# Laying HGRN's work slots as one list over two pairs of heads, and weighting slot positions by chunk

## The reference

```python
h = rms_norm(x, norm_mix) * (1.0 + sc_a) + sh_a
z = h @ w_in
q, k, v, rq, rf, ri, rg, ga, gr = split(z)
...
o_attn = sliding_window_attention(q, k, v)      # 16 heads, 4 kv heads, window 128, sinks, ALiBi
o_rec, s_new = hgrn2_chunked(qr, kr, vr, logf, s0)   # 8 heads, 128x128 state each
mixed = sigmoid(ga) * o_attn + sigmoid(gr) * o_rec
x = x + g_a * (mixed @ w_out)
x = x + g_m * (square(relu(h2 @ w_up)) @ w_down)
```

## Time and profile before

| | |
|---|---|
| time, median of 3 runs | 1206.25 us (1203.26 to 1206.48) |
| the profiled execution | 1207.19 us, span of its instructions 1205.4 us |
| TensorE | busy 1136.0 us (94% of the span), mean granted clock 0.972 |
| VectorE, ScalarE, GpSimd | busy 706.4, 530.5, 174.1 us |
| stretch that holds the slots | about 94 us to 674 us of the span |

### The profile page before, as it was taken

The page is one execution under the profiler, slowest core; times in us unless marked ns, Lnnn a source line. Parts: engine busy times, 40 slices in busy tenths (PEclk is TensorE's granted clock), DMA queues, the critical chain, the costliest instruction groups (busy, mean ns, idle before and its releaser), DMA issues.

```text
span 1205.4 us, 22012 instructions
## 1 busy us (share of the span) xinstructions
PE 1136.0 (94%) x8837; PEld 1073.0 (89%) x8837; DVE 706.4 (59%) x1437; ACT 530.5 (44%) x939; POOL 174.1 (14%) x137
## 2 busy tenths in 40 slices
PE   5798999997999989999999999799999999999997
PEld 4687889885899988989999999589999999999997
DVE  5635555545386677376688654744553744636465
ACT  3432556466546555555536423443323233232324
POOL 1300000000142123122031001231001010110101
PEclk9899999998999989999999999799999999999999
DMA  9684432312232312213222265112222222232212
GB/s 301 201 302 154 136 106 71 107 36 70 109 94 73 108 38 71 72 50 95 76 68 73 91 236 157 36 46 95 71 96 80 72 87 89 71 104 71 71 36 79
DMA packets 108779, 120.46 MB, mean 100 GB/s; under 512 B 2693, under 2 KB 98653, under 8 KB 108390
## 3 DMA queue, kind: packets, MB, share of 16 engines
q1 hardware_dynamic: 108677, 119.06, 30.4%
HBM read 109.22 MB, written 11.80 MB: 100 GB/s over the span
## 4 chain that ended last, share of the span: by engine, by line
PE 44%; DVE 4%; ACT 1%; issue 1%; POOL 0%; DVEq 0%; ACTq 0%; POOLq 0%
PE PS L834 40%; DVE wR L1408 1%; DVE tmp L1392 1%; DVE xhat L1376 1%; PE PS L956 0%; PE PS L747 0%; PE PS L1002 0%; PE PS L1019 0%; PE PS L780 0%; DVE tmp L1391 0%; DVE xT L1425 0%; PE PS L843 0%; ACT wR L1079 0%; DVE xT L1426 0%; PE PS L986 0%
## 5 line engine op out<-in xcount | busy, mean ns | idle before, releaser
L834 PE MATMUL PS<-hR,wR 128*128 128x288 f32 x3744 | 530.9, 300 | 0.8 <-issue 0.8
L834 PEld LDWEIGHTS PS<-hR,wR 128*128 128x128 f32 x3744 | 508.1, 190 | 10.3 <-issue 9.5
L834 PE MATMUL PS<-actR,wR 128*128 128x288 f32 (+2 forms) x1920 | 259.3, 295 | 1.8 <-DVE actR L1556 1.8
L834 PEld LDWEIGHTS PS<-actR,wR 128*128 128x128 f32 x1920 | 255.5, 188 | 3.0 <-DVE actR L1556 2.0
L1408 DVE TENSOR_TENSOR wR<-raw,wR 128x512 fp32r<-128x512 f32 x256 | 209.1, 817 | 81.1 <-ACT wR L1079 74.1
L1079 ACT ACTIVATE wR<-raw 128x512 fp32r<-128x512 f32 x256 | 161.8, 632 | 140.5 <-PE PS L834 132.9
L1741 POOL TENSOR_TENSOR D<-b 128x512 f32<-128x512 f32 (+1 forms) x48 | 60.4, 1257 | 490.6 <-PE PS L921 263.6
L1471 DVE CAST actR<-tmp 128x576 fp32r<-128x576 f32 x32 | 15.2, 476 | 129.5 <-ACT tmp L1190 129.5
L1768 POOL TENSOR_TENSOR actR<-tmp,actR 128x576 fp32r<-128x576 f32 x32 | 46.3, 1448 | 304.7 <-DVE actR L1471 304.7
L789 PE MATMUL PS<-wR,hR 128*128 128x256 f32 x600 | 80.6, 292 | 2.2 <-ACT kT L1159 2.2
L789 PEld LDWEIGHTS PS<-wR,hR 128*128 128x128 f32 x600 | 75.8, 196 | 4.7 <-ACT kT L1159 2.4
(11 more groups left out here) (223 smaller groups left out, 1233.3 us busy)
## 6 DMA issues: line engine op xcount, KB each, us to landing
raw<-in_w_in SPq DMA_DIRECT2D x30, 1024.0 KB, 5.1
raw<-in_w_up SPq DMA_DIRECT2D x16, 1024.0 KB, 5.5
raw<-in_w_down SPq DMA_DIRECT2D x16, 1024.0 KB, 5.0
mid<-in_w_ada SPq DMA_DIRECT2D x12, 1024.0 KB, 5.0
ada<-in_w_ada SPq DMA_DIRECT2D x8, 1024.0 KB, 12.4
S<-in_state_hgrn SPq DMA_DIRECT2D x8, 512.0 KB, 4.2
out_hgrn_sample<-S SPq DMA_DIRECT2D x8, 512.0 KB, 5.0
raw<-in_w_out SPq DMA_DIRECT2D x4, 1024.0 KB, 5.3
```

The costliest lines, as they stand in the source:

```text
L834: mm = pe.matmul(PS[:, 2 * x.pair + h, 0:size], weights(x, w, k, col), rhs[r], start=(k == 0 and n == 0), stop=(k == last and n == 2))
```

## The change

The function that lays slots now counts room: a chunk has room 2, a chunk of a unit of kind ri has room 1, and slots are spread evenly over the sum of the room. The HGRN slots of pairs 0 and 1 are laid as one list over ga 0 to ri 2, those of pairs 2 and 3 as one list over rf 3 to rg 2. The slots, their events and their order stay as they are.

```diff
-        slots, chunks = list(slots), [(x.t, c) for x in TILES[begin:end] if x.u not in MID for c in range(parts(x))]
-        for n, ev in enumerate(slots):
-            plan.setdefault(chunks[n * len(chunks) // len(slots)], []).extend(ev)
+        slots, at = list(slots), 0
+        chunks = [(x, c) for x in TILES[begin:end] if x.u not in MID for c in range(parts(x))]
+        room = [1 if x.kind == "ri" and CHUNKS.get("ri") == 2 else 2 for x, _ in chunks]
+        for (x, c), r in zip(chunks, room):
+            for n in range(-(-at * len(slots) // sum(room)), -(-(at + r) * len(slots) // sum(room))):
+                plan.setdefault((x.t, c), []).extend(slots[n])
+            at += r
...
     spread(attention_slots(), first["q", 1], first["ga", 0])
-    spread(hgrn_slots(0), first["ga", 0], first["rf", 2])
-    spread(hgrn_slots(1), first["rf", 2], first["rf", 3])
-    spread(hgrn_slots(2), first["rf", 3], first["gr", 1])
-    spread(hgrn_slots(3), first["gr", 1], first["gr", 3])
+    spread([*hgrn_slots(0), *hgrn_slots(1)], first["ga", 0], first["rf", 3])
+    spread([*hgrn_slots(2), *hgrn_slots(3)], first["rf", 3], first["gr", 3])
```

## The result

The kernel after takes 1223.82 us in the median of 4 runs (1223.73 to 1224.08), against 1206.37 us (1203.26 to 1209.05) before in the same comparison: a ratio of 1.015, 95% interval 1.013 to 1.017. It is slower, by 17 us. The forecast was 1203.8 us, so it was wrong, and the range did not hold the time.

What follows compares the result with a forecast made beforehand. TensorE bounds the kernel, so only waits and granted clock can change. Attention +2.5, heads 0 to 3 -4.0 and heads 4 to 7 -1.0 sum to -2.5 us: 1203.8 us, own range 1200 to 1210, 8-in-10 range 1196.5 to 1212.5.

Steps and rivals of the forecast that it cites:

- the guest at 30.1: Attention: slots follow each other at 28.2 and 28.3 and 30.0 is now empty, so this guest waits 1.5 us more.
- the first sample step: Attention: it moves from 31.3 to 31.0, before `q_blocks` has ended, and TensorE waits 1.0 us more.
- tile 43: Attention, rf 1 and rq 1: with one slot more, waits of about 2.0, 0.7 and 0.9 us here.
- The two waits of the earlier trace: Heads 0 to 3: the waits of 2.73 us at 63.2 and 2.04 us at 66.1 both go.
- levels 1, 2, 3 of head 1: Heads 0 to 3, in ga at 57.1 to 57.3, all with `lo`: a new wait of 1.5 us.
- levels 2 to 4 of head 2: Heads 0 to 3, at 61.1 to 61.3, again with `lo`: a new wait of 1.0 us.
- head 3 behind the scans: Heads 0 to 3: head 3 stands behind the scans of rf 2, a new wait of 1.0 us.
- The rate 1.5: Heads 0 to 3: the 1.5 us charged for three neighbouring levels with `lo` in ga, the shape of 66.1.
- I move 2 of the 2.7 us: Heads 4 to 7: of the 2.67 us wait at 73.0, 2 us pass from level 3 of head 4 to level 4.
- Head 7's wait: Heads 4 to 7: head 7 starts at 87.2, with the merge and `lo` in the same chunk, and may wait 2 us.
- Waits move, the sum stays: First rival, the forecast itself: removed waits have near twins, time within -3.6 and +3.6 us; chance 0.42.
- Rival 3: Slower: attention's loop no longer catches up in rf and rq, +8.5 us, 1214.8 us; chance 0.22.

Runs made afterwards that it cites:

- e1: Kernel after with attention's slots laid as before (equal room), HGRN's as changed: 1219.58 us, ratio 1.0122 to the kernel before.
- e2: Kernel after with HGRN's slots laid as before, attention's still weighted: 1210.23 us, ratio 1.0034 to the kernel before.
- e5: Kernel after with one slot, level 5 of head 4, moved one chunk later from 73.1 to 73.2: 1216.78 us, ratio 1.0086 to the kernel before.
- e3: Kernel after with the joined HGRN lists kept but equal room for every chunk, attention too: 1216.21 us, ratio 1.0087 to the kernel before.
- e4: Kernel after with four separate HGRN lists, ri still at room 1, attention at equal room: 1208.39 us, ratio 1.002 to the kernel before.
- e6: Kernel after with attention and pairs 2 and 3 as before, pairs 0 and 1 separate and weighted: 1202.44 us, ratio 0.996 to the kernel before.
- e7: Kernel after with attention and pairs 2 and 3 as before, pairs 0 and 1 joined with equal room: 1205.91 us, ratio 0.9993 to the kernel before.
- e8: Plan of the kernel before with the slots of pairs 2 and 3 one chunk later: 1209.85 us, ratio 1.0025 to the kernel before.
- e11: Plan of the kernel before with all attention slots one chunk later, room equal: 1209.26 us, ratio 1.0035 to the kernel before.
- e9: Pairs 0 and 1 separate and weighted, rest as before, plus three slots at waits (73.0, 85.1, 88.0) one chunk later: 1203.18 us, ratio 0.998 to before.
- e10: Kernel after with five slots of heads 1 to 3, at or right behind its large waits, one chunk later: 1223.58 us, ratio 1.0146 to the kernel before.

## Why the prediction was wrong

**Bound.** That only waits and clock can change was right: the constant part of each stretch is the same before and after, to 0.6 us. SyncE's transfers, costed at nothing, cost nothing: no wait of TensorE in these stretches ends with a transfer, before or after. That one wait more counts nearly double, because of the clock, does not hold for the sum: 15.7 us of waits came with 1.7 us of clock.

**Attention, +2.5 forecast, +3.9 measured.** The mechanism was right, the list of waits was short, and part of the agreement is luck: waits were to rise by 1.5 us and rose by 7.1, while the clock, put at 1.0 us of loss more, lost 3.4 us less. As forecast, TensorE waits at 22.0 (2.67 for 3.08 us, gain 0.4 of 0.5), the guest at 30.1 waits (1.33 against 1.5), the first sample step waits (0.63 against 1.0), tile 43 waits (2.25, 0.93, 1.34 against 2.0, 0.7, 0.9), the guest of tile 45 waits (1.79 against 1.2) and its sum does not. Missing were the 2.48 us at 292.87, in the same unit, where the step-by-step chain stopped one slot too early, and the 1.26 and 1.84 us at 145.29 and 165.34, each at the second of two neighbouring slots: 28.3, and 26.1, which lies in the second tile of a unit, where the forecast priced neighbours at nothing. Of the 1.7 us that ri 0 and ri 1 were to give back 0.6 came: a wait of 1.12 us at 241.36 is new. The sum of waits was 22.2 us, past the 22 that were named as a sign of error. e1 and e2 put the price of this part at about 4 us both ways, e2 with 1.7 to 6.5 us as its interval.

**Heads 0 to 3, -4.0 forecast, +4.1 measured: the first failed step.** The two waits of the earlier trace rows did go. The waits forecast in their place were in the right places and too small: "levels 1, 2, 3 of head 1" 1.5 against 2.21, "levels 2 to 4 of head 2" 1.0 against 2.25, "head 3 behind the scans" 1.0 against 3.62 + 1.03. In all 11.0 instead of 4.0 us, and 6.3 us before. The clock, of which 1.3 us were to come back, gave back nothing. The sign for it, a wait of over 2 us in ga, came up. The rate 1.5 was read from one place (66.1, 2.04 us) and shaded down, though ga has GpSimd's long instructions beside the products; the forecast had that price and set it off as covered.

**Heads 4 to 7, -1.0 forecast, +9.4 measured: the step that cost most.** "I move 2 of the 2.7 us" from level 3 to level 4 at 73.0: it was level 5 at 73.1, with 2.95 us, after two small ones and before the 1.51 us of `qs`. Head 7's wait was forecast at 2 and was 1.53. Waits rose by 3.9 us where they were to fall by 1.0, and "clock unchanged" was +5.1 us, three pieces. e5 shows both to hang largely on one slot: one chunk later gives 8.3 us of the stretch back. e3 and e4 show which half of the edit brings it: the joined lists give 218.9 and 220.6 us with either weight, separate ones 209.5 to 213.3. Not joining as such, though: e5 is joined too, and takes 210.6.

**The weights.** The premise that a room of one half is wrong for ri stands (1.67 against 1.83 us). But I leaned on it as a fault of the change, and by itself it isn't: weighted and separate, heads 0 to 3 are the fastest of all (160.4 us, e4, e6). It costs only together with the joined list, 7.7 us there (168.6 against 160.9 us, e3).

**The rivals.** "Waits move, the sum stays" is wrong: the twins were larger than what they replaced. Rival 3 had the sign, but the wrong place: attention gave 3.9 of 16.7 us. I take the tails to have been too thin because each moved wait was given a spread of its own, and none for the clock: with 1.7 us a piece and some ten pieces in play, three more are within reach of any plan.

**What stays open.** Why in heads 0 to 3 weighting alone saves 4.1 us and joining alone 2.1 to 3.6 (e7, e3), and both together cost 4.1, is measured and not explained. I found no simple count of the plan (levels in the first tiles of units, neighbouring levels, filled chunks per unit) that orders the kernels. Which later slot brings the other pieces of clock that e5 also removed, well behind the moved one, is open too.

## What to carry to other kernels

A plan that lays work of one in-order stream between that of another by a formula is judged by its worst collisions, not by its density: one slot one chunk later was worth 7 us of 1224 (e5), and a shift of one part's slots by one chunk 3 to 4 (e8, e11). But to move the slots at the waits that one sees is no cure by itself: in e9 and e10 the waits went on to the next levels. Price a long wait of TensorE with the half-speed work that can follow it, and try parts of such a change separately: here the part that only reweighted pairs 0 and 1 was faster by 0.4% (0.2 to 0.6%), inside a change that was slower by 1.5%.

## What the runs showed of the hardware

Half-speed work came in pieces that each cost 1.70 to 1.72 us, in every kernel here. In HGRN's stretches of the 14 traces TensorE waits 58 times for 1.5 us or more (to 4.21 us); at 43 of them half speed begins in the wait or within 2 us behind it. Filling one such wait (2.95 to 1.04 us) removed two pieces. Others come with no long wait near: in the kernel after, the low windows that start at 443, 594 and 642 us come with or right behind the block of small matmuls of `g_out` (L1000 to L1004: 32 matmuls of 128 columns or fewer, 16 of them of 8). The 14 traces hold 112 such blocks, and behind 35 of them half speed begins within 2 us. These 43 and 35 are all 78 times that half speed begins in HGRN's stretches. That long waits bring it is shown by the filled one; for the block there is only the coincidence, and why it brings half speed in one case in three is not shown. Why a plan with equal waits has two pieces in one profile and three in another is not shown.
